# A decoder layer on one core: the FFN's second product by nine pairs of row blocks in place of six, with the weight sums made by accumulating DMAs in DRAM

## The reference

```python
h = rmsnorm(x, norm_mix_pre[layer])
... # q, k, v, gates = h @ w_in, split
merged = (g[:, :, 0] * (o_a @ w_branch_a[layer])
          + g[:, :, 1] * (o_b @ w_branch_b[layer])
          + g[:, :, 2] * (o_c @ w_branch_c[layer]))
x = x + rmsnorm(merged @ w_out[layer], norm_mix_post[layer])
h = rmsnorm(x, norm_ffn_pre[layer])
gate, up = jnp.split(h @ w_ffn_in[layer], 2, axis=-1)
x = x + rmsnorm((jax.nn.silu(gate) * up) @ w_ffn_out[layer], norm_ffn_post[layer])
```

## Time and profile before

| | |
|---|---|
| time, median of 3 (lowest, highest) | 915.83 us (915.33, 916.66) |
| the profiled execution's own time | 916.67 us |
| its span | 914.9 us |
| mean granted TensorE clock | 0.996 of full speed |
| matmuls | 5254 |
| DMA traffic | 113.67 MB, mean 124 GB/s |

### The profile page before, as it was taken

One profiled execution on the slowest core, in us unless ns is written; L12 is line 12 of the kernel. 1 busy time (PEld: TensorE's weight loads), 2 busy tenths in 40 slices (PEclk: granted clock), 3 DMA queues, 4 the chain that ended last, 5 costly groups with the idle time before them and its releaser, 6 DMA issues.

```text
span 914.9 us, 14398 instructions
## 1 busy us (share of the span) xinstructions
PE 907.7 (99%) x5254; PEld 800.4 (87%) x5254; DVE 635.7 (69%) x1175; ACT 488.4 (53%) x926; POOL 158.8 (17%) x168
## 2 busy tenths in 40 slices
PE   9999999999999999999999999999999999999997
PEld 8888888888888888888888888989999999988886
DVE  5998655462555555656567758768888888769787
ACT  6744245343556665667664535435556555424762
POOL 3000263344133433434410001000000000000000
PEclk9999999999999999999999999999999999999999
DMA  9323626222323232274337843113322322480002
GB/s 346 125 73 88 199 92 223 77 93 93 99 85 104 82 109 94 92 274 123 107 107 264 308 139 115 47 46 105 127 94 95 134 95 93 141 342 24 1 24 92
DMA packets 37602, 113.67 MB, mean 124 GB/s; under 512 B 4324, under 2 KB 6948, under 8 KB 36780
## 3 DMA queue, kind: packets, MB, share of 16 engines
q1 hardware_dynamic: 36700, 109.08, 34.5%
q10 hardware_dynamic: 832, 3.67, 1.3%
HBM read 98.87 MB, written 13.66 MB: 123 GB/s over the span
## 4 chain that ended last, share of the span: by engine, by line
PE 98%; DMA 1%; DVE 0%; SPq 0%; ACT 0%; DVEq 0%; issue 0%
PE bank L2207 28%; PE bank L2208 28%; PE bank L2209 27%; PE bank L821 3%; PE bank L813 2%; PE bank L838 2%; PE bank L836 2%; PE bank L812 2%; PE bank L2272 1%; PE bank L2226 1%; DMA xT<-x_features 1%; PE bank L2401 0%; PE bank L752 0%; PE bank L2459 0%; PE bank L2322 0%; PE bank L2388 0%
## 5 line engine op out<-in xcount | busy, mean ns | idle before, releaser
L1095 ACT ACTIVATE w_hi<-w_raw 128x1024 fp32r<-128x1024 f32 (+1 forms) x90 | 94.7, 1054 | 129.2 <-PE bank L2209 125.9
L2207 PE MATMUL bank<-h_hi,w_lo 128*128 128x512 f32 x352 | 140.6, 400 | 0.0
L2208 PE MATMUL bank<-h_lo,w_hi 128*128 128x512 f32 x352 | 138.2, 393 | 0.0
L2209 PE MATMUL bank<-h_hi,w_hi 128*128 128x512 f32 x352 | 137.9, 392 | 0.0
L1511 DVE TENSOR_TENSOR w_lo<-w_raw,w_hi 128x1024 fp32r<-128x1024 f32 (+1 forms) x69 | 84.3, 1223 | 42.1 <-ACT w_hi L1095 41.7
L705 DVE CUSTOM_DVE_ANT_0 sc<-bank,fullb 128x512 f32<-128x512 f32 (+1 forms) x96 | 47.0, 489 | 77.8 <-PE bank L813 76.0
L605 ACT ACTIVATE sc<-sc,ast 128x512 f32<-128x512 f32 (+1 forms) x96 | 53.9, 561 | 72.8 <-DVE ast L705 72.8
L1037 POOL TENSOR_TENSOR sc<-sc,ast 128x512 f32<-128x512 f32 (+1 forms) x96 | 66.2, 721 | 130.7 <-DVE ast L727 97.8
L2208 PE MATMUL bank<-tx_lo,op_hi 128*128 128x256 f32 x288 | 81.5, 283 | 0.0
L2209 PE MATMUL bank<-tx_hi,op_hi 128*128 128x256 f32 x288 | 81.5, 283 | 0.0
L2207 PE MATMUL bank<-tx_hi,op_lo 128*128 128x256 f32 x288 | 81.5, 283 | 0.0
(11 more groups left out here) (380 smaller groups left out, 2439.4 us busy)
## 6 DMA issues: line engine op xcount, KB each, us to landing
w_raw<-wpack SPq DMA_DIRECT2D x132, 512.0 KB, 3.6
gate_logits<-gl_out SPq DMA_DIRECT2D x24, 256.0 KB, 2.2
gl_in<-gate_logits SPq DMA_DIRECT2D x24, 256.0 KB, 4.8
dn_sw<-wpack SPq DMA_DIRECT2D x4, 1536.0 KB, 9.4
near_bias<-near_bias ACTq DMA_DIRECT2D x1, 2880.0 KB, 13.7
xT<-x_features SPq DMA_DIRECT2D x8, 256.0 KB, 5.8
xs<-x_in SPq DMA_DIRECT2D x4, 512.0 KB, 8.8
fullb<-near_bias SPq DMA_DIRECT2D x16, 128.0 KB, 2.8
```

The source lines that it names most:

```text
L1095: sa.activation(split_weights(c)[0][:, 0:n], raw[:, s, 0:n], ACT.Copy).then_inc(w_hi, 1)
L2207: mm(out, ll, rh, start=start, stop=False, skip_group_check=True)
L2208: mm(out, lh, rl, start=False, stop=False, skip_group_check=True)
L2209: return mm(out, lh, rh, start=False, stop=stop, skip_group_check=True)
```

## The change

The last 18 blocks of the FFN's second product, not 12, go through the seven products: nine pairs in three groups of three; four blocks stay plain. The weight sums t1 to t4 are no longer made by VectorE. They are made in DRAM: the weights of the pairs are packed so that b11, b12, b21, b22 of all nine pairs are each one flat stretch, and GpSimd issues 72 DMAs of 256 KB each (8 steps x 9 pairs), 36 plain copies DRAM to DRAM and 36 that add their source to what stands in DRAM. One is issued ahead of `scale(u)` in nine of every eleven attention units from unit 3 on; the first of a step waits until all nine of the step before have landed. Signs of some activation sums are turned for this, with the joins to match (s1 and s4, `sixth_into_c12`, `c22`).

The right operands are no longer resident: SP loads each of the 21 (768 KB) in a ring of five buffers, the first five as soon as the product s4 of the last first-product pair is done, each later one when the operand five before it is multiplied. The high parts rotate through five buffers instead of four. VectorE makes the nine sums s1, s2, s3 before the first low part, and s4 after the sixth.

```diff
-DOWN_PAIRS = 3
+DOWN_PAIRS, DOWN_GROUPS = 3, 3
+N_DOWN = DOWN_PAIRS * DOWN_GROUPS
-F_DOWN = NF - 4 * DOWN_PAIRS
+F_DOWN = NF - 2 * N_DOWN
+BLOCK = P * 512
+SUM_STEPS = (("t1", "b11", False), ("t3", "b12", False), ("t1", "b12", True), ("t3", "b22", True),
+             ("t2", "t3", False), ("t2", "b11", True), ("t4", "t2", False), ("t4", "b21", True))
+SUMS_FROM, SUMS_EVERY = 3, N_DOWN + 2
+RIGHT_RAW, DOWN_HI = 5, 5
...
+        def right_landed(eng, o):
+            eng.wait_ge(load_in[o % RIGHT_RAW], 16 * (o // RIGHT_RAW + 2))
...
@@ SP
+            def load_right(o):
+                i, g = divmod(o, DOWN_GROUPS)
+                if o >= RIGHT_RAW:
+                    sp.wait_ge(dn_done, operand_done(o - RIGHT_RAW))
+                mine = down_blocks[DOWN[i][1]][g * DOWN_PAIRS * BLOCK:(g + 1) * DOWN_PAIRS * BLOCK]
+                sp.dma_start(dn_right[o % RIGHT_RAW][:, :, :], mine.rearrange("(j p n) -> p j n", j=DOWN_PAIRS, p=P)
+                             ).then_inc(load_in[o % RIGHT_RAW], 16)
...
-            sp.wait_ge(op_used, N_OPERANDS)
-            load_group(0)
-            fetch(C_FOUT + 6)
-            load_group(1)
-            for c in range(C_FOUT + 7, C_DOWN):
-                fetch(c)
+            sp.wait_ge(op_used, used_at(operand(N_PAIRS - 1, "s4")))
+            sp.wait_ge(sums_in, 16 * N_DOWN * len(SUM_STEPS))
+            for o in range(4 * DOWN_GROUPS):
+                load_right(o)
...
@@ GpSimd
+            def down_copy(name, of, q):
+                mine = slice(q * BLOCK, (q + 1) * BLOCK)
+                pool.dma_start(down_blocks[name][mine], down_blocks[of][mine], max_dma_last_dim=8192).then_inc(sums_in, 16)
+
+            def down_add(name, of, q):
+                mine = slice(q * BLOCK, (q + 1) * BLOCK)
+                pool.dma_start(down_blocks[name][mine], down_blocks[of][mine], accum_op=ALU.add, max_dma_last_dim=8192
+                               ).then_inc(sums_in, 16)
+
+            def down_sums(u):
+
+                step, q = divmod(u - SUMS_FROM, SUMS_EVERY)
+                if not (0 <= step < len(SUM_STEPS) and q < N_DOWN):
+                    return
+                if q == 0 and step > 0:
+                    pool.wait_ge(sums_in, 16 * N_DOWN * step)
+                name, of, adds = SUM_STEPS[step]
+                if adds:
+                    down_add(name, of, q)
+                else:
+                    down_copy(name, of, q)
+
             for u in range(len(UNITS) + 8):
+                down_sums(u)
                 if u < len(UNITS):
                     scale(u)
...
@@ ScalarE
-            down_high(0)
-            down_high(1)
+            for o in range(2):
+                down_high(o)
             for i, b in enumerate((2, 3, 4, 5)):
                 keep(i, b)
-            down_high(2)
-            down_high(3)
-            down_high(4)
+            for o in range(2, 7):
+                down_high(o)
             copy_out(0, 0, 2)
...
@@ VectorE
-            between = {2: DOWN_SUMS[0:2], 3: DOWN_SUMS[2:5], 4: DOWN_SUMS[5:8], 5: DOWN_SUMS[8:10], 6: DOWN_SUMS[10:12],
-                       7: DOWN_SUMS[12:14], 8: DOWN_SUMS[14:16]}
             for k in range(2, F_DOWN):
                 act_lo(k)
                 lo(C_FOUT + k)
-                for name, g in between.get(k, ()):
+                if k == 2:
+                    for g in range(DOWN_GROUPS):
+                        down_sum("s1", g)
+            for name in ("s2", "s3"):
+                for g in range(DOWN_GROUPS):
                     down_sum(name, g)
-            for o in range(5):
+            for o in range(6):
                 down_low(o)
+            for g in range(DOWN_GROUPS):
+                down_sum("s4", g)
             first_into_c11(0)
             first_into_c11(1)
```

More of the change, by code:

```diff
@@ L313, in program @@
[L313 to L319, removed]
@@ new lines, in program @@
+        dnh_left = [at(195 + 3 * k, f"dn_left_hi{k}", [P, DOWN_PAIRS, 256], F32R) for k in range(4)]
+        dnh_left.append(at(60, "dn_left_hi4", [P, DOWN_PAIRS, 256], F32R))
+        dnh_right = [at(144 + 6 * k, f"dn_right_hi{k}", [P, DOWN_PAIRS, 512], F32R) for k in range(4)]
+        dnh_right.append(at(40, "dn_right_hi4", [P, DOWN_PAIRS, 512], F32R))
+        kept = [at(120 + 2 * i, f"kept{i}", [P, SEQ]) for i in range(4)]
+        copied = [at(32 + 2 * i, f"copied{i}", [P, SEQ]) for i in range(4)]
@@ L333, in program @@
         upper = at(204, "upper", [P, 3, 256])
[L336 to L337 removed]
+        small_in, sums_in = sem("small_in"), sem("sums_in")
+        load_in = [sem(f"load_in{k}") for k in range(NT + 1)]
         xr_in, posts_in, stored = sem("xr_in"), sem("posts_in"), sem("stored")
@@ L994, in _ @@
             sp.dma_start(wfpost[:, :], rows_d[2, :, :]).then_inc(posts_in, 16)
+            for o in range(4 * DOWN_GROUPS, DOWN_GROUPS * len(DOWN)):
+                load_right(o)
             for t in range(NT):
@@ L1456, in _ @@
             z_square(1, 1)
-            down_high(12)
+            for o in range(17, 20):
+                down_high(o)
             z_square(0, 0)
             z_square(1, 0)
-            down_high(13)
+            down_high(20)
             copy_out(5, 0, 2)
@@ L2176, in _ @@
             z_weight(1, 1)
-            down_low(12)
+            for o in range(17, 20):
+                down_low(o)
             z_mean(0)
@@ L2181, in _ @@
             z_weight(1, 0)
-            down_low(13)
+            down_low(20)
             z_out(0, slice(0, D))
@@ L2612, in down_block @@
                 left, right = DOWN[i]
-                o = 2 * i + g
-                high, low = dnh_left[o % 4], down_left(left, g, True)
-                wide, narrow = dnh_right[o % 4], down_right(right, g, True)
+                o = DOWN_GROUPS * i + g
+                high, low = dnh_left[o % DOWN_HI], down_left(left, g, True)
+                wide, narrow = dnh_right[o % DOWN_HI], dn_right_low[o % RIGHT_RAW]
                 out = bank[(2, 4, 2, 4, 0, 2, 2)[i] + m]
@@ L2635, in _ @@
             for m in range(2):
-                for g in range(2):
+                for g in range(DOWN_GROUPS):
                     down_block(len(DOWN) - 1, g, m)
@@ L2695, in pack_weights @@
         out.append(tiles(a["w_ffn_in"][0][:, HID * side + P * f:HID * side + P * f + P]))
-    rows = list(range(F_DOWN))
-    rows += [F_DOWN + 2 * (DOWN_PAIRS * g + j) + k for g in range(2) for k in range(2) for j in range(DOWN_PAIRS)]
-    for k in rows:
+    for k in range(F_DOWN):
         out.append(a["w_ffn_out"][0][P * k:P * k + P])
+    blocks = a["w_ffn_out"][0][P * F_DOWN:].reshape(N_DOWN, 2, P, 2, 512).transpose(1, 3, 0, 2, 4)
+    out.extend(np.ascontiguousarray(blocks).reshape(2 * N_DOWN, P, CHUNK))
     for c, m in enumerate(out):
```

140 lines of the change are left out of this document (58 added, 82 removed).

## The result

| | before | changed |
|---|---|---|
| time, median (lowest to highest), same chip | 915.58 us (915.26 to 916.66), 4 runs | 923.46 us (921.47 to 924.65), 4 runs |
| ratio | | 1.0077, 95% interval 1.006 to 1.0093 |
| profiled execution, its span | 916.67 us, 914.9 us | 924.65 us, 922.9 us |

The change makes the kernel 7.9 us slower; 912.0 was predicted. (One execution of one kernel of the experiments took 1509.85 us at a mean granted clock of 0.556, and is in no median or ratio here.) Against the sum some 11.5 us had to be found, and the page of the changed kernel says at once that they are not work. It is the page's busy line, its chain and its line for GpSimd's DMA queue (compare).

What follows compares the result with a forecast made beforehand. TensorE was taken as the bound: number of matmuls times their pace. 916.67 - 4.08 (matmuls) + 0.3 (seam), all else nothing, gave 912.9 us for the profiled execution, so a median of 912.0, range 911.0 to 914.5.

Steps and rivals of the forecast that it cites:

- Matmuls: TensorE's second product: 18 fewer matmuls (492 to 474) at 0.2267 us each, 4.08 us less.
- The seam: Where TensorE passes from plain blocks to pairs: a wait of 0.3 us for `down_low(0)`, bounds 0 and 1.0.
- GpSimd's price of an issue, c: Time one DMA issue occupies GpSimd in attention: 1.0 to 1.3 us, hidden in idle time, cost nothing.
- rival B: GpSimd falls behind in attention: issues cost over 1.65 us each, TensorE waits at the transposes, kernel slower; chance 0.15.
- its second way: GpSimd's issues in attention held up by VectorE: half a microsecond more on 1.2 is just the edge.
- The ring: Right operands' loads for the pairs: 5 us a load, 7 us left over, cost nothing; stalls only above 12.2 us.
- twelve matmuls: Start of the first five loads: s4 of the last pair done, twelve matmuls before 796.19, about 794.8.
- The queues behind these waits are in order: ScalarE's and VectorE's work behind the ring's waits: `copy_out` and `down_low(15)` needed only 12 us later; cost nothing.
- The full stretch: Attention up to 412, DMA engines full: four or five sum DMAs delay the swapped keys; nothing taken, bound 2 us.
- Rival C: Small waits of 1 to 2 us at the swapped keys or the seam, 913 to 915 us; chance 0.14.
- The end: Program's end: 5.9 us after the start of TensorE's last matmul, as before; no term in the sum.
- The sum: Whole kernel: 916.67 - 4.08 + 0.3 = 912.9 us for an execution like the profiled one, median 912.0.

Runs made afterwards that it cites:

- the kernel with 24 DMAs: The kernel with both edits, its weight sums made by 24 DMAs of 768 KB in place of 72 of 256 KB; 912.17 us, ratio 0.9955.
- both edits: The changed kernel with `plain_into_c21(0)` moved ahead of `down_low(20)` and no sum DMAs in attention units 62 to 73; 914.87 us, ratio 0.999.

## Why the prediction was wrong

*Matmuls (-4.08): right.* 18 fewer; the 378 of the pairs go from 818.81 to 904.44 in the kernel with 24 DMAs, 0.2271 a step.

*The seam (+0.3): right, a little high.* In the changed kernel the first pair starts 0.253 us after the matmul before it, where the pace is 0.227, and the next two, the first of which needs the right low part, 0.341 and 0.240 after that: 0.15 in all. VectorE was as near the limit as the working said: `down_low(0)` ends at 824.35 for a start at 824.41.

*GpSimd's price of an issue, c, 1.0 to 1.3: too high, and harmless.* GpSimd's busy time is 158.7 us without sums, 175.0 with 24 DMAs and 211.5 with 72 (both edits made): 0.68 and 0.73 for an issue. Between two scales a copying issue takes 0.54. The adding ones are less even: 0.79 to 2.30 us in the changed kernel, median 1.08, and ten of the 36 took over 1.3, two of them beyond the 1.6 that the prediction named. The two longest had a `w_lo` of VectorE beside them (one in the fence), which is what rival B names as its second way, but few did and the slack held. A scale of 128 columns, 0.42 otherwise, took 1.88 there.

```profile
342.85 1.88 POOL L1045 TENSOR_TENSOR sc<-sc,ast 128x128 f32<-128x128 f32 x1
343.20 2.29 POOL L1070 DMA_DIRECT2D down_sums<-wpack  x1
343.26 1.23 DVE L1536 TENSOR_TENSOR w_lo<-w_raw,w_hi 128x1024 fp32r<-128x1024 f32 x1
```

Rival B, which held all of the chance for slower, did not happen: no transpose waited for GpSimd. That the kernel came out slower is thus not what that chance stood for.

*The ring (0): right about the loads, wrong about the queue.* A load took 4.5 us (5 taken). The first one went out at 799.89, 1.24 us before the first plain matmul, as the prediction's 794.8 says, although "twelve matmuls" would be 2.7; the five landed in 14 us, not 12, the first at 804.29 and thus in time. The step that failed is the sentence that begins "The queues behind these waits are in order". It went through `copy_out`, `c12` and `down_low(15)`, and left out `plain_into_c21(0)` behind `down_low(20)`. The load for operand 20 can start only when operand 15 is done, two operands before the last product; 4.8 + 1.5 + 2.6 + 1.2 + 0.7 = 10.8 us later the join is done, and TensorE wanted it after 8.0 (from 890.04 to 898.02). In before no load stood in this chain: ScalarE was done with `down_high(13)` 3.3 us before it copied the bank, and the same order cost nothing, with little in hand: the join ended at 900.53 and TensorE started on its bank at 901.03. Price in the profile of the changed kernel: 3.0 us and 1.7 of clock, 4.7; by medians 4.1 to 6.1.

*The full stretch (0, bound 2 us): the step that failed first in the order of time.* Place and mechanism were those named. The working counted the four or five DMAs behind 408 and not those of units 62 to 69, which fed the same backlog: the engines are full from 393, not from 400. The wait was 1.9 us in the profile of the changed kernel, inside the bound, but 3.3 in two other profiles, and in one of these a half-speed stretch behind it cost 3.0 more. By medians the stretch's DMAs cost 2.5 to 4.5 us in the changed kernel and 6.8 on the kernel before. Rival C had the wait at 1 to 2 us and ended at 915.

*The end (5.9 us behind the last matmul, "as now"): the third step that failed.* It was no term at all, and the end lay 8.2 us behind: 2.2 for the drain. No row of before could show a drain that grows by 0.08 us a DMA; but its 0.65 us and the 3.7 us between its end and SyncE's stood in the trace, and would have said up to where a longer one is hidden.

*The sum.* From the medians: the changed kernel lost 8.6 us against the one with both edits, and this one 2.7 against that with fewer DMAs: 923.5 - 8.6 - 2.7 = 912.2. That it meets the prediction's 912.0 so closely is partly luck, since the executions behind each median scatter by 2 us and more. What is not the change's is in it: the four executions of the changed kernel were probably a little slow, by the stretch at half clock near 175, whose length was 3.4 us, 6.8 us or nothing in the profiles of kernels that are the same program up to there. Their mean granted clocks speak for it: 0.995 in the fastest (921.47 us) and 0.992 in the slowest (924.65), and 0.003 of 920 us is 2.8 of the 3.2 us between them. What decides that, and why a wait of 3.3 us for the keys brought half clock in one profile and not in another, stays open.

## What to carry to other kernels

When a deep chain (here a ring of loads) is put into a queue in order, list every instruction behind each wait up to the end of the program, and ask of the last ones above all who wants them first: one join of 0.7 us behind an operand that nobody needed yet cost 4.7. Extra DMAs can be hidden over 200 us at a mean DMA share of 0.76 and still cost time in the 30 us in which the engines are full; a backlog must be added up from the point at which it begins, and work that has free choice of time keeps out of that stretch. And look at the end of the span, by engine: what each engine must still do after its last instruction is a slack like any other.

## What the runs showed of the hardware

- GpSimd's closing drain grows with the number of DMAs that it has issued, about 0.08 us each (0.651, 0.747, 2.626 and 6.546 us for 0, 1, 24 and 72), long after the last of them has landed, and not with bytes.
- An issue of 768 KB holds GpSimd no longer than one of 256 KB: 0.68 us against 0.73.
- VectorE and GpSimd held each other up. A `w_lo` of VectorE (two operands in SBUF, 128x1024) takes 1.23 us alone; one that met a head's low part on GpSimd (`L1050`) took 2.37 in the kernel with both edits (first fence). In the changed kernel a low part, which takes 1.29 alone, began just behind a `w_lo` and took 2.35 (second fence). In both the one that began first kept its usual time, and the two together took 2.38 and 2.39 us.

```profile
331.10 2.37 DVE L1538 TENSOR_TENSOR w_lo<-w_raw,w_hi 128x1024 fp32r<-128x1024 f32 x1 [0.99 <-ACT w_hi L1128]
...
331.09 1.29 POOL L1050 TENSOR_TENSOR oa<-tmp,oa 64x512 fp32r<-64x512 f32 x1
```

```profile
335.19 1.23 DVE L1536 TENSOR_TENSOR w_lo<-w_raw,w_hi 128x1024 fp32r<-128x1024 f32 x1 [0.99 <-ACT w_hi L1126]
...
335.23 2.35 POOL L1050 TENSOR_TENSOR oa<-tmp,oa 64x512 fp32r<-64x512 f32 x1
```

The Trainium skill (SBUF — State Buffer, section "SBUF: two separate sides") calls this an exclusive lock on a shared pair of ports, held for a whole instruction; the trace agrees to within 0.2 us (1.29 + 1.23 is 2.52). GpSimd's copying DMAs issued inside a `w_lo` took their usual 0.54 us, so those issues were not held up by it; of the adding ones some took up to 2.30.
- The Trainium skill (DMA: Bandwidth & Descriptors, "Queues, rings and completion order") has each DMA engine take turns between the queues that have work for it. The swap's 10.33 us fit with this: when it was issued, some 3 MB of SyncE's queue and three of GpSimd's sum DMAs had not landed, and three more sum DMAs, issued after it, landed before it. No run here tells turns from another way of sharing.
